# A hybrid retention and attention block: two projections run side by side, two steps moved to GpSimd, the last stage pipelined

## The chip, the cores and the metric

The kernel runs on one core of a Trainium2 chip. A core has five engines that work at the same time: TensorE (PE, matrix products into PSUM), VectorE (DVE), ScalarE (ACT), GpSimd (POOL) and SyncE (SP, which issues most of the DMAs). They are ordered among themselves only by semaphores. The metric is the device time of one execution, in microseconds (us). Lower is better.

## The reference, cut to what matters

One decoder block on `x` of 512 tokens by 1024 columns, in f32:

```
mod = silu(c) @ w_ada + b_ada                    # 6 groups of 1024: sh1 sc1 ga1 sh2 sc2 ga2
h   = rmsnorm(x) * (1 + sc1) + sh1
(retention q, k, v, gate; attention q; compressed k, v; selected k, v; window k, v; 24 gates) = split(h @ w_in)
y_ret = retention(rope(rq), rope(rk), rv) * silu(rg)        # 4 heads, y / rms(y) per head
y_nsa = g0 * o_compressed + g1 * o_selected + g2 * o_window # 8 heads in 2 groups
x = x + ga1 * (concat(y_ret, y_nsa) @ w_out)
h2 = rmsnorm(x) * (1 + sc2) + sh2
x = x + ga2 * ((silu(h2 @ w_gate) * (h2 @ w_up)) @ w_down)
out = rmsnorm(x) * ln_final_g
```

## The kernel before, in words

Tokens are tiled by 128 (TT = 4 tiles), model columns by 128 (KT = 8), FFN columns by 128 (FT = 22). Every large product is made of three fp32r products (`product`: high by high, high by low, low by high), so each weight tile must be split: ACT copies `raw` into `wh` (`high`, L456), POOL subtracts to get `wl` (`low`, L404). The work is counted in units: 24 units of `w_in`, 8 of `w_out`, 44 of gate and up, 22 of down. A unit of `w_in` is two of the eight k tiles (a "quarter") of one of six column chunks. The chunks follow each other: CMP (compressed keys and values, selected keys and values, 512 columns), Q (512), RQK (512), WIN (window keys and values and the gates, 280), RG (512), RV (512). Unit v of the loop `for v in range(U_IN)` is chunk v // 4, quarter v % 4. Each engine has its own copy of this loop, with its side work hung in at fixed v, so the order is written out by hand on every engine, and each engine works strictly in that order.

Quarter q of chunk CMP needs h for k = 2q, 2q+1, and h needs sc1 and sh1 for these columns. So w_ada's first two groups come in quarters: SP streams four `early` tiles and one `w_in` unit per quarter; DVE adds the `early` tiles up with the weights silu(c) (`ada_early`, L713 and L716, 16 operations of 256 columns per quarter); PE sums over partitions (`modulation`, in its queue in the middle of the unit before, ahead of token tile 2); DVE turns the sums into `mods`; ACT makes `hf` (L488) and `hTh` (L491); DVE makes `hTl` (`h_low`, L770); then PE can start the quarter.

The other four groups of w_ada (sc2, ga1, sh2, ga2: operations 16 to 47, one k tile of 1024 columns each, `ada`, L729 and L732) share the ring of seven `raw` tiles with the weight units. `stream()` spreads them over 20 units; DVE works them at v = u - 3 behind the rest of v. `sum_rows` (PE, L1180, one call is two matmuls) gives the rows ga1 and ga2, `mod_rows` (DVE, L765) adds the bias. A raw tile is refilled when its last reader is done.

At set places the evacuated projections are rotated (`rope_chunk`, DVE L808 to L811, per token tile), transposed (`rot_transposes`, PE L1201, L1206), and split again (`rot_high` on ACT, `rot_low` on DVE, L846, L849). `pairs_transposes` (PE) and `pairs_copy` (ACT, L530) lay out the compressed branch, whose small MLP runs behind unit 14 (L1399).

Attention and retention run in 42 slots (`for n in range(SLOTS)`), with tables that name the slot of each side task: scores (PE), exp (ACT), values (PE, L1274), row minima (`row_min`, DVE L875), and
- `add_branch` (DVE L894 to L901): 1/denominator, times gate, `tmpo` from PSUM (L896), then `mix += tmpo` (L901);
- `ret_norm` (DVE): `tmpo` = y * rstd from PSUM (L948), then `mix` = 0.5 * tmpo * gate (L950);
- `mix_transposes` and `out_unit` on PE: `w_out` follows, then the FFN, two matmul groups per f, then the down product.

In the last stage, per token tile: DVE adds the product to `x1` (L1122, two halves), ACT squares with a running sum (L689), DVE makes the variance (L1124, L1125), multiplies the first half by g (L1127), POOL raises to the power -0.5 (L409), DVE scales both halves (L1130, L1131), SP writes 512 KB. DVE does tile t wholly before tile t + 1.

Of the kernel before, what the change touches and what calls it, by code (L numbers as in the profile page):

```python
# [34 lines left out]
CHUNKS = [(C_CMP, 512), (C_Q, 512), (C_RQK, 512), (C_WIN, 280), (C_RG, 512), (C_RV, 512)]  # L35
K_CMP, K_Q, K_RQK, K_WIN, K_RG, K_RV = range(6)
# [46 lines left out]

def stream():

    items = []
    for q in range(UPC):
        items += [("early", 4 * q + j) for j in range(4)] + [("w", q)]
    a = ADA_START
    for u in range(3, UNITS):  # L90
        if u > 3:
            items.append(("w", u))
        upto = min(KT * len(ADA), ADA_START - (-(KT * len(ADA) - ADA_START) * (u - 2) // ADA_UNITS))
        while a < upto:
# [5 lines left out]
def block_kernel(nc, x, c, ln_mix_g, ln_ffn_g, w_ada, b_ada, w_in, cmp_pe_k, cmp_w1_k, cmp_w2_k,  # L100
# [17 lines left out]
    with ExitStack() as ctx:
# [1505 lines left out]
```

## Time and profile before

| | us |
|---|---|
| median of 3 runs | 727.98 |
| lowest and highest | 725.49, 729.76 |
| the profiled execution's own time | 729.54 |
| its span, first to last instruction | 727.7 |

| engine | busy us | share of the span | instructions |
|---|---|---|---|
| PE matmul | 682.1 | 94% | 3547 |
| PE weight load | 564.1 | 78% | 3547 |
| DVE | 332.8 | 46% | 587 |
| POOL | 265.9 | 37% | 127 |
| ACT | 225.5 | 31% | 378 |

How to read it: a matmul's end is modelled and overlaps the next one's start, so PE's busy share says less than the distance from one start to the next. DVE's 46% is a mean: it is over 90% from 60 to 150 us and mostly under 20% in the FFN. "L404" is line 404 of kernel.py. In rows of the timeline the columns are start, duration, engine, line, operation, output<-inputs, their shapes, count, and in brackets the idle time before and who ended it. Rows of the table of stretches are: stretch, its length, then busy us and (count) of PE, PEld, DVE, ACT, POOL (PE and PEld alone where one line was asked for), the granted share of TensorE's clock, the DMA engines' busy share, and GB/s.

### The profile page before, as it was taken

Reading aid. Unit: us, or ns where it says so; the run is one execution under the profiler, and the core shown is the slowest. Engines: PE = TensorE matmul, PEld = TensorE weight load, DVE = VectorE, ACT = ScalarE, POOL = GpSimd, SP = SyncE. Lnnn points to the kernel's source line nnn. Section 1 sums busy time; section 2 is a strip of 40 time slices with the busy share of each in tenths; the row PEclk is TensorE's granted clock in tenths of the full one; section 3 lists DMA queues with packets and bytes.
Section 4 is the critical chain, followed back from the end, with each engine's and each line's share of the span. In section 5 each row is a group of like instructions: output and inputs, shape, how many; then the busy total and the mean of one; then the engine's idle time right before and its main releaser. Section 6 shows DMA issues by size and latency. Waiting matters only on the chain.

```text
span 727.7 us, 9019 instructions
## 1 busy us (share of the span) xinstructions
PE 682.1 (94%) x3547; PEld 564.1 (78%) x3547; DVE 332.8 (46%) x587; ACT 225.5 (31%) x378; POOL 265.9 (37%) x127
## 2 busy tenths in 40 slices
PE   2678899999989898999999999999999999999995
PEld 1556679987768687888898888888888888888884
DVE  4878999977465668152620110000000029633126
ACT  4435233422132333332542222222222213232222
POOL 2316443432000111138034434434434427545531
PEclk9699999999998899999999999999999999999999
DMA  9975986665000000176014233233233223232002
GB/s 314 359 257 152 353 293 234 199 240 228 30 2 1 0 2 1 40 221 202 1 48 127 87 96 107 87 98 104 87 102 101 89 86 117 86 103 72 0 1 116
DMA packets 73962, 88.09 MB, mean 121 GB/s; under 512 B 3048, under 2 KB 57536, under 8 KB 73792
## 3 DMA queue, kind: packets, MB, share of 16 engines
q1 hardware_dynamic: 73184, 86.36, 36.0%
q0 software_dynamic: 416, 1.08, 0.4%
q8 instruction: 28, 0.46, 0.3%
q14 instruction: 14, 0.11, 0.0%
q10 hardware_dynamic: 320, 0.07, 0.0%
HBM read 85.41 MB, written 2.10 MB: 120 GB/s over the span
## 4 chain that ended last, share of the span: by engine, by line
PE 78%; DVE 10%; ACT 3%; issue 3%; DMA 3%; SPq 2%; POOL 0%; POOLq 0%; DVEq 0%
PE ps L1523 11%; PE ps L1524 11%; PE ps L1522 11%; PE ps L1141 11%; PE ps L1143 11%; PE ps L1142 11%; PE ps L1274 3%; DMA raw<-in_w_in 3%; DVE acc L732 2%; DVE ps L875 1%; SPq L344 1%; PE ps L1332 1%; PE ps L1399 1%; PE ps L1228 1%; ACT hf L488 1%
## 5 line engine op out<-in xcount | busy, mean ns | idle before, releaser
L404 POOL TENSOR_TENSOR wl<-raw,wh 128x1024 fp32r<-128x1024 f32 (+1 forms) x94 | 238.6, 2543 | 285.8 <-ACT wh L456 285.6
L456 ACT ACTIVATE wh<-raw 128x1024 fp32r<-128x1024 f32 (+1 forms) x94 | 97.4, 1039 | 154.4 <-PE ps L1524 73.9
L1522 PE MATMUL ps<-hTh,wh 128*128 128x512 f32 (+1 forms) x384 | 142.8, 372 | 0.0
L1523 PE MATMUL ps<-hTl,wh 128*128 128x512 f32 (+1 forms) x384 | 142.6, 371 | 0.0
L1524 PE MATMUL ps<-hTh,wl 128*128 128x512 f32 (+1 forms) x384 | 142.6, 371 | 0.0
L1106 DVE TENSOR_TENSOR act<-ps,sg 128x512 f32<-128x512 f32 x22 | 15.2, 692 | 212.3 <-PE ps L1524 212.3
L1141 PE MATMUL ps<-wh,hTh 128*128 128x512 f32 (+1 forms) x224 | 90.5, 404 | 11.8 <-DVE hTl L770 10.6
L1143 PE MATMUL ps<-wh,hTl 128*128 128x512 f32 (+1 forms) x224 | 85.8, 383 | 0.0
L1142 PE MATMUL ps<-wl,hTh 128*128 128x512 f32 (+1 forms) x224 | 85.7, 383 | 0.0
L1522 PEld LDWEIGHTS ps<-hTh,wh 128*128 128x128 f32 x384 | 72.4, 188 | 12.5
L1523 PEld LDWEIGHTS ps<-hTl,wh 128*128 128x128 f32 x384 | 72.4, 188 | 12.4
L1524 PEld LDWEIGHTS ps<-hTh,wl 128*128 128x128 f32 x384 | 72.4, 188 | 12.4
L1141 PE MATMUL ps<-wh,ah 128*128 128x512 f32 x176 | 68.5, 389 | 0.0
L1142 PE MATMUL ps<-wl,ah 128*128 128x512 f32 x176 | 68.5, 389 | 0.0
L1143 PE MATMUL ps<-wh,al 128*128 128x512 f32 x176 | 68.5, 389 | 0.0
L1141 PEld LDWEIGHTS ps<-wh,hTh 128*128 128x128 f32 x224 | 43.0, 192 | 23.9 <-issue 8.3
L732 DVE SCALAR_TENSOR_TENSOR acc<-raw,cs,acc 128x1024 f32<-128x1024 f32 x28 | 53.3, 1904 | 1.8
L1143 PEld LDWEIGHTS ps<-wh,hTl 128*128 128x128 f32 x224 | 43.0, 192 | 8.3
L1142 PEld LDWEIGHTS ps<-wl,hTh 128*128 128x128 f32 x224 | 43.2, 193 | 7.8 <-issue 1.0
L799 DVE TENSOR_TENSOR raw<-raw,ga 128x1024 f32<-128x1024 f32 x30 | 46.8, 1585 | 0.0
L1101 DVE TENSOR_TENSOR al<-act,ah 128x512 fp32r<-128x512 f32 x22 | 19.5, 888 | 50.5 <-ACT ah L667 50.5
L1274 PEld LDWEIGHTS ps<-V,PT 128*128 128x128 f32 x320 | 38.1, 195 | 5.4 <-DVE tmpo L896 3.2
(197 smaller groups left out, 818.4 us busy)
## 6 DMA issues: line engine op xcount, KB each, us to landing
raw<-in_w_ada SPq DMA_DIRECT2D x32, 512.0 KB, 5.8
raw<-in_w_ff_gate SPq DMA_DIRECT2D x22, 512.0 KB, 3.8
raw<-in_w_ff_up SPq DMA_DIRECT2D x22, 512.0 KB, 3.7
raw<-in_w_ff_down SPq DMA_DIRECT2D x22, 512.0 KB, 3.2
raw<-in_w_in SPq DMA_DIRECT2D x20, 512.0 KB, 7.0
early<-in_w_ada SPq DMA_DIRECT2D x16, 512.0 KB, 9.6
raw<-in_w_out SPq DMA_DIRECT2D x8, 512.0 KB, 6.6
xs<-in_x SPq DMA_DIRECT2D x4, 512.0 KB, 5.3
```

The lines of the kernel that those rows point to most:

```text
L404: pool.tensor_tensor(lo, raw[:, slot, 0:n], hi.bitcast(F32), ALU.subtract).then_inc(w_lo, 1)
L456: a.activation(split(u, n)[0], raw[:, slot, 0:n], ACT.Copy).then_inc(w_hi, 1)
L732: d.scalar_tensor_tensor(dst, raw[:, slot, :], cs[:, k:k + 1], dst, ALU.mult, ALU.add).then_inc(ada_used, 1)
L799: d.tensor_tensor(raw[:, slot, :], raw[:, slot, :], ga[:, :], ALU.mult).then_inc(w_scaled, 1)
L1101: d.tensor_tensor(al[:, f % SPLIT, :], act[:, f, :], ah[:, f % SPLIT, :].bitcast(F32), ALU.subtract).then_inc(a_lo, 1)
L1141: mm(o, ah_, bh_, start=first, stop=False)
L1142: mm(o, ah_, bl_, start=False, stop=False)
L1143: return mm(o, al_, bh_, start=False, stop=last)
L1274: ins = mm(ps[:, 2 + g, h * DE:(h + 1) * DE], PT[:, n % 2, g, h * P:(h + 1) * P], V[:, j, b, g, :], start=j == 0 and h == 0, stop=j == i a ...
L1522: mm(o, hi[:, ks], hTh[:, k, c0:c1], start=k == 0, stop=False)
L1523: mm(o, hi[:, ks], hTl[:, k, c0:c1], start=False, stop=False)
L1524: ins = mm(o, lo[:, ks], hTh[:, k, c0:c1], start=False, stop=k == KT - 1)
```

## The change

The parts are:
1. Chunk WIN now runs with CMP: units 0 to 7 are CMP and WIN in turn for each quarter (`chunk_of`), WIN in PSUM banks 4 and 5, so four chunks follow instead of five. Token tile 3 of WIN is split into two products of 128 and 152 columns for lack of room in one bank. Both units of a quarter's weights are streamed with its `early` tiles. ACT's `high` of the next quarter stands behind the second `hTh`, no longer between the first and the second.
2. `ada_early` takes two tiles in one operation of 512 columns: 8 per quarter instead of 16, each waiting for the one before.
3. Keys of CMP and WIN are rotated together; the transposes of Q and RQK move: the second pair of Q stands behind unit 14 (the unit after the first pair), the MLP follows.
4. Groups sc2, ga1, sh2 of w_ada spread over 14 units from unit 8 on; group ga2 (8 operations) moves to the FFN, one per f from f = 2 to 9, with its `sum_rows` behind gate and up of f = 11 and 12.
5. In attention, `mix += tmpo` and the retention gate are POOL's; POOL's `low` of the first w_out units is put into the slots with them. `add_branch` on DVE stands first in its slot. The retention's factor 0.5 goes into the variance.
6. Last stage: DVE finishes tile t - 1 behind the first half of tile t; the last tile in three pieces; each half is written by its own DMA, one from SP and one from ACT.

The diff, cut to its core ("..." is what is left out):

```diff
-CHUNKS = [(C_CMP, 512), (C_Q, 512), (C_RQK, 512), (C_WIN, 280), (C_RG, 512), (C_RV, 512)]
+CHUNKS = [(C_CMP, 512), (C_WIN, 280), (C_Q, 512), (C_RQK, 512), (C_RG, 512), (C_RV, 512)]
-OUT_AT = {16: 0, 20: 1, 26: 2, 30: 3}
+OUT_AT = {14: 0, 18: 1, 31: 2, 33: 3}
-ADA_UNITS = 20
+ADA_UNITS = 14
+ADA_LAST = 5 * KT
+ADA_FFN = U0_GU + 8
+def chunk_of(u):
+    return (u % 2, u // 2) if u < 2 * UPC else divmod(u, UPC)
...
@@ gpsimd
+            def add_branch(x):
+                i, b = divmod(x, 2)
+                pool.wait_ge(o_read, x + 1)
+                pool.wait_ge(c_mix, i + 1)
+                y = mix[:, i % 2, 512:1024]
+                pool.tensor_tensor(y, y, tmpo[:, :], ALU.add).then_inc(b_mix, 1)
+                pool.wait_ge(b_mix, x + 1)
+            def ret_gate(i):
+                pool.wait_ge(r_half, i + 1)
+                pool.tensor_tensor(mix[:, i % 2, 0:512].rearrange("p (h x) -> p h x", h=RH), normed_y(i),
+                                   rg[:, i, :].rearrange("p (h x) -> p h x", h=RH), ALU.mult).then_inc(r_norm, 1)
+            def attention():
+                for n in range(SLOTS):
+                    if n % 2 and n // 2 in STEP0[1:]:
+                        add_branch(STEP0.index(n // 2) - 1)
+                    if n in SQ_AT:
+                        power(N_RET + SQ_AT[n], yss[:, :])
+                    if n in NORM_AT:
+                        ret_gate(NORM_AT[n])
+                    if n in OUT_AT:
+                        low(U0_OUT + OUT_AT[n])
...
@@ scalar
             for k in range(KT):
-                if k % 2 and k < KT - 1:
-                    high(k // 2 + 1)
...
                 a.activation(hTh[:, k, :], hf[:, k % 2, :], ACT.Copy).then_inc(h_hi, 1)
+                if k % 2 and k < KT - 1:
+                    high(k + 1)
+                    high(k + 2)
...
@@ vector
-                    dst = acc[:, i, 2 * q * P:2 * (q + 1) * P]
-                    src = early[:, j % EARLY, 2 * kk * P:2 * (kk + 1) * P]
+                    dst = acc[:, :, 2 * q * P:2 * (q + 1) * P]
+                    src = early[:, j % EARLY:j % EARLY + 2, 2 * kk * P:2 * (kk + 1) * P]
...
-                d.wait_ge(o_read, x + 1)
-                d.wait_ge(c_mix, i + 1)
-                y = mix[:, i % 2, 512:1024]
-                d.tensor_tensor(y, y, tmpo[:, :], ALU.add).then_inc(b_mix, 1)
-                d.wait_ge(b_mix, x + 1)
...
-                then(d.tensor_tensor(heads_view(tmpo[:, :], RH), heads_view(ps[:, 7, :], RH),
-                                     yss[:, :].unsqueeze(2).broadcast_to([P, RH, RDV]), ALU.mult))
-                d.scalar_tensor_tensor(mix[:, i % 2, 0:512], tmpo[:, :], 0.5, rg[:, i, :], ALU.mult, ALU.mult).then_inc(r_norm, 1)
-                d.wait_ge(r_norm, i + 1)
+                if i:
+                    d.wait_ge(r_norm, i)
+                d.tensor_tensor(normed_y(i), heads_view(ps[:, 7, :], RH),
+                                yss[:, :].unsqueeze(2).broadcast_to([P, RH, RDV]), ALU.mult).then_inc(r_half, 1)
...
-                for n in {7: [0], 10: [1, 2], 12: [3, 4], 19: [9]}.get(v, []):
+                for n in {11: [0, 1], 14: [2, 3], 15: [4, 5]}.get(v, []):
                     rot_low(n)
...
+                if f == 12:
+                    mod_rows(9, ga2, 0, bank=4)
+                if f == 13:
+                    mod_rows(10, ga2, 1, bank=5)
...
             for t in range(TT):
+                last = len(PIECES[t]) - 1
+                take(t, 0)
+                scale_final(t, 0)
+                if t:
+                    finish(t - 1)
+                then(variance_final(t, 0))
...
@@ tensor
-                    pe.wait_ge(rot_lo, min(n - 1, 5))
+                    pe.wait_ge(rot_lo, min(n - 1, 6))
...
-                    pe.wait_ge(r_norm, i)
+                    pe.wait_ge(r_half, i)
...
-                for m in {6: [0], 9: [1, 2], 11: [3, 4], 13: [5, 6], 15: [7, 8], 18: [9]}.get(v, []):
+                for m in {10: [0, 1], 13: [2, 3], 14: [4, 5], 17: [6, 7], 18: [8, 9]}.get(v, []):
                     rot_transposes(m)
...
-                if v == 17:
+                if v == 18:
+                    pe.wait_ge(mod_read, 7)
                     pe.wait_ge(ada_used, ada_ops(5 * KT - 1))
                     sum_columns(0, 40, range(KT)).then_inc(mod_sum, 1)
...
+                if f == 11:
+                    sum_rows(5, 0, bank=4)
+                if f == 12:
+                    pe.wait_ge(mod_read, 9)
+                    sum_rows(5, 1, bank=5)
```

The order on three engines, before and after. First ACT at the start of the projection, before: one weight copy (`wh<-raw`) stands between the two activations of a quarter.

```order
L488 ACTIVATE hf<-xT,mods 128x512
L491 ACTIVATE hTh<-hf 128x512
L456 ACTIVATE wh<-raw 128x1024
L488 ACTIVATE hf<-xT,mods 128x512
L491 ACTIVATE hTh<-hf 128x512
```

ACT after, at the same quarter:

```order
L541 ACTIVATE hf<-xT,mods 128x512
L544 ACTIVATE hTh<-hf 128x512
L541 ACTIVATE hf<-xT,mods 128x512
L544 ACTIVATE hTh<-hf 128x512
L510 ACTIVATE wh<-raw 128x1024
L510 ACTIVATE wh<-raw 128x560
```

The weight copies, now two per quarter, moved behind the second `hTh`.

DVE before, from the last rotated tile of Q to the first two `QTl` (`rot_low`):

```order
L808 TENSOR_TENSOR rt<-stage,cst 128x512
L809 TENSOR_TENSOR rt<-stage,cst 128x8x32
L810 TENSOR_TENSOR rt<-stage,cst 128x8x32
L811 TENSOR_TENSOR rot<-rt 128x2x4x64
L732 SCALAR_TENSOR_TENSOR acc<-raw,cs,acc 128x1024
L849 SCALAR_TENSOR_TENSOR QTl<-ps,QTh 128x4x128 x2
```

DVE after, the same place:

```order
L876 TENSOR_TENSOR rt<-stage,cst 128x512
L877 TENSOR_TENSOR rt<-stage,cst 128x8x32
L878 TENSOR_TENSOR rt<-stage,cst 128x8x32
L879 TENSOR_TENSOR rot<-rt 128x2x4x64
L800 SCALAR_TENSOR_TENSOR acc<-raw,cs,acc 128x1024 x2
L908 SCALAR_TENSOR_TENSOR QTl<-ps,QTh 128x4x128 x2
```

Two `ada` operations stand in front of the first `QTl` where one stood.

POOL before, from the window's last units to the end of attention:

```order
L404 TENSOR_TENSOR wl<-raw,wh 128x1024 x4
L409 TENSOR_TENSOR yss<-yss,expo 128x4 x2
L404 TENSOR_TENSOR wl<-raw,wh 128x1024 x2
L409 TENSOR_TENSOR yss<-yss,expo 128x4
L404 TENSOR_TENSOR wl<-raw,wh 128x1024 x2
L409 TENSOR_TENSOR yss<-yss,expo 128x4
L404 TENSOR_TENSOR wxl<-raw,wxh 128x1024 x4
```

POOL after, the first rows of the same stretch:

```order
L430 TENSOR_TENSOR wl<-raw,wh 128x1024 x2
L435 TENSOR_TENSOR yss<-yss,expo 128x4
L443 TENSOR_TENSOR mix<-mix,tmpo 128x512
L448 TENSOR_TENSOR mix<-hTf,rg 128x512
L443 TENSOR_TENSOR mix<-mix,tmpo 128x512 x2
L435 TENSOR_TENSOR yss<-yss,expo 128x4
L443 TENSOR_TENSOR mix<-mix,tmpo 128x512
L448 TENSOR_TENSOR mix<-hTf,rg 128x512
L430 TENSOR_TENSOR wl<-raw,wh 128x1024 x2
L443 TENSOR_TENSOR mix<-mix,tmpo 128x512
```

Twelve operations of 512 columns (8 `mix<-mix,tmpo`, 4 `mix<-hTf,rg`) are new on POOL, between the powers and the `low` of w_out.

## Rows read from the trace of the kernel before

**Rows 1.** The page: busy time of each engine.

```profile
PE 682.1 (94%) x3547; PEld 564.1 (78%) x3547; DVE 332.8 (46%) x587; ACT 225.5 (31%) x378; POOL 265.9 (37%) x127
```

**Rows 2.** The table of stretches: start-up, projections, attention.

```profile
13.40:66.50 53.10, 39.59 (x160) 29.64 (x161) 43.16 (x88) 24.84 (x39) 16.92 (x7) 0.84 0.80 269
66.50:200.40 133.90, 130.90 (x716) 109.13 (x717) 112.94 (x201) 40.92 (x84) 44.75 (x21) 1.00 0.64 225
200.40:309.50 109.10, 101.69 (x758) 82.66 (x756) 63.45 (x151) 35.57 (x85) 13.55 (x8) 0.94 0.03 8
```

**Rows 3.** Timeline of DVE and ACT in the start-up.

```profile
39.54 1.92 DVE L770 TENSOR_TENSOR hTl<-hf,hTh 128x512 fp32r<-128x512 f32 x1 [0.84 <-ACT hTh L491]
41.38 2.85 DVE L716 SCALAR_TENSOR_TENSOR acc<-early,cs,acc 128x256 f32<-128x256 f32 x7
50.55 0.69 DVE L770 TENSOR_TENSOR hTl<-hf,hTh 128x512 fp32r<-128x512 f32 x1 [0.84 <-ACT hTh L491]
...
59.55 0.69 DVE L770 TENSOR_TENSOR hTl<-hf,hTh 128x512 fp32r<-128x512 f32 x1 [0.68 <-ACT hTh L491]
...
48.10 1.04 ACT L456 ACTIVATE wh<-raw 128x1024 fp32r<-128x1024 f32 x1
```

**Rows 4.** Timeline: DVE beside POOL, with two SBUF inputs and with one.

```profile
140.07 3.52 DVE L732 SCALAR_TENSOR_TENSOR acc<-raw,cs,acc 128x1024 f32<-128x1024 f32 x1
...
140.10 2.40 POOL L404 TENSOR_TENSOR wl<-raw,wh 128x1024 fp32r<-128x1024 f32 x1
...
119.88 1.29 DVE L849 SCALAR_TENSOR_TENSOR QTl<-ps,QTh 128x512 fp32r<-128x512 f32 x2 [0.63 <-ACT QTh L541]
...
119.42 1.40 POOL L404 TENSOR_TENSOR wl<-raw,wh 128x560 fp32r<-128x560 f32 x1 [4.05 <-ACT wh L456]
```

**Rows 5.** Table of stretches, L1141 alone: one 512-column unit, one WIN unit.

```profile
72.44:78.00 5.56, 3.21 (x8) 1.47 (x8) 1.00 0.96 316
118.72:122.00 3.28, 2.40 (x8) 1.47 (x8) 1.00 0.94 335
```

**Rows 6.** Timeline of PE: a sum of rows, the small MLP.

```profile
93.49 1.02 PE L1180 MATMUL ps<-acc,ones 128*128 128x512 f32 x2
...
131.17 8.00 PE L1399 MATMUL ps<-pairsT,w 128*128 128x66 f32 x64
```

**Rows 7.** Waits of PE, 66.5 to 200 us: waiter, releaser, total, times, longest.

```profile
PE ps L1190 <- ACT pairsT L530: 2.0, 1, 2.0
```

**Rows 8.** Timeline of DVE from Q's evacuation to its `rot_low`.

```profile
94.55 0.69 DVE L765 TENSOR_TENSOR ga<-ps,ga 128x512 f32<-128x512 f32 x1
...
95.76 2.62 DVE L809 TENSOR_TENSOR rt<-stage,cst 128x256 f32<-128x256 f32 x1
...
110.39 1.28 DVE L732 SCALAR_TENSOR_TENSOR acc<-raw,cs,acc 128x1024 f32<-128x1024 f32 x1
111.59 1.28 DVE L849 SCALAR_TENSOR_TENSOR QTl<-ps,QTh 128x512 fp32r<-128x512 f32 x2
```

**Rows 9.** Groups by shape, 200.4 to 309.5 us: busy us, mean ns, idle before.

```profile
L404 POOL TENSOR_TENSOR wl<-raw,wh 128x1024 fp32r<-128x1024 f32 x4 | 9.5, 2372 | 38.3 <-ACT wh L456 38.3
...
L901 DVE TENSOR_TENSOR mix<-mix,tmpo 128x512 f32<-128x512 f32 x7 | 4.8, 691 | 0.2
...
L950 DVE SCALAR_TENSOR_TENSOR mix<-tmpo,rg 128x512 f32<-128x512 f32 x4 | 2.8, 692 | 0.1
```

**Rows 10.** The last tile's drain: timeline of PE, DVE and POOL, and the DMA.

```profile
718.49 0.39 PE L1143 MATMUL ps<-wh,al 128*128 128x512 f32 x1
...
719.89 1.28 DVE L1122 TENSOR_TENSOR x<-ps,x 128x512 f32<-128x512 f32 x2
...
722.40 0.92 POOL L409 TENSOR_TENSOR rstd<-rstd,expo 128x1 f32<-128x1 f32 x1 [3.68 <-DVE rstd L1125]
...
723.84 0.74 DVE L1131 SCALAR_TENSOR_TENSOR xb<-x,rstd,gfin 128x512 f32<-128x512 f32 x1
...
out<-xb SPq DMA_DIRECT2D x4, 512.0 KB, 2.6
```

More of the change, by code:

```diff
@@ L87, in stream @@
     for q in range(UPC):
-        items += [("early", 4 * q + j) for j in range(4)] + [("w", q)]
+        items += [("early", 4 * q + j) for j in range(4)] + [("w", 2 * q), ("w", 2 * q + 1)]
     a = ADA_START
-    for u in range(3, UNITS):
-        if u > 3:
+    for u in range(2 * UPC - 1, UNITS):
+        if u >= 2 * UPC:
             items.append(("w", u))
-        upto = min(KT * len(ADA), ADA_START - (-(KT * len(ADA) - ADA_START) * (u - 2) // ADA_UNITS))
+        if u < ADA_FFN:
+            upto = min(ADA_LAST, ADA_START - (-(ADA_LAST - ADA_START) * (u - 2 * UPC + 1) // ADA_UNITS))
+        else:
+            upto = min(KT * len(ADA), ADA_LAST + (u - ADA_FFN) // 2 + 1)
         while a < upto:
@@ L207, in block_kernel @@
         ssq = small("ssq", [P, TT])
-        ssq2 = small("ssq2", [P, TT])
+        part = small("part", [P, 3])
         rstd = small("rstd", [P, TT])
@@ L414, in _ @@
             for u in range(UNITS):
-                for i in {U0_OUT: (0, 1), U0_OUT + 2: (2,), U0_OUT + 4: (3,)}.get(u, ()):
-                    power(N_RET + i, yss[:, :])
+                if u == U0_OUT:
+                    attention()
+                if U0_OUT <= u < U0_OUT + len(OUT_AT):
+                    continue
                 if u == U0_GU + SPLIT:
@@ L1004, in _ @@
                     cmp_scores(0)
-                    mod_rows(9, ga2, 0)
                     for h in range(HPG):
@@ L1010, in _ @@
                     cmp_gates(0)
-                    mod_rows(10, ga2, 1)
                     row_min(2, 0)
@@ L1022, in _ @@
                     ada(j)
-            for h in range(HPG):
-                row_min(3, h)
+            row_min(3, 0)
+            row_min(3, 1)
             cmp_gates(1)
+            row_min(3, 2)
+            row_min(3, 3)
             for n in range(SLOTS):
+                if n % 2 and n // 2 in STEP0[1:]:
+                    add_branch(STEP0.index(n // 2) - 1)
                 for x, h in PAIR_AT.get(n, []):
@@ L1031, in _ @@
                     max_rows(MAX_AT[n])
-                if n % 2 and n // 2 in STEP0[1:]:
-                    add_branch(STEP0.index(n // 2) - 1)
                 if n in CS_AT:
@@ new lines, in scale_final, with variance_final @@
+            def scale_final(t, n):
+                c0, c1 = PIECES[t][n]
+                if t >= 2 and n == 0:
+                    d.wait_ge(out_done[t - 2], 32)
+                d.wait_ge(x2_ok, piece_count(t, n))
+                d.tensor_tensor(xb[:, t % 2, c0:c1], x1[:, t, c0:c1], gfin[:, c0:c1], ALU.mult).then_inc(y_scaled, 1)
+            def variance_final(t, n):
+                d.wait_ge(sq3, piece_count(t, n))
+                v = rstd[:, t:t + 1]
+                if n == 0:
+                    return d.tensor_scalar(v, part[:, 0:1], 1.0 / D, EPS, ALU.mult, ALU.add)
+                return d.scalar_tensor_tensor(v, part[:, n:n + 1], 1.0 / D, v, ALU.mult, ALU.add)
@@ new lines, in finish @@
+            def finish(t):
+                d.wait_ge(rstd_ok, N_X2 + t)
+                d.wait_ge(y_scaled, piece_count(t, 0))
+                d.tensor_scalar(xb[:, t % 2, 0:HALF], xb[:, t % 2, 0:HALF], rstd[:, t:t + 1], None, ALU.mult).then_inc(y_ok, 1)
+            for t in range(TT):
+                last = len(PIECES[t]) - 1
+                take(t, 0)
+                scale_final(t, 0)
+                if t:
+                    finish(t - 1)
+                then(variance_final(t, 0))
+                for n in range(1, last + 1):
+                    take(t, n)
+                for n in range(1, last + 1):
+                    if n == last and last > 1:
+                        then(variance_final(t, 1))
+                    scale_final(t, n)
+                variance_final(t, last).then_inc(var_ok, 1)
@@ L1135, in _ @@
+            finish(TT - 1)
         @block.tensor
```

264 lines of the change are left out of this document (137 added, 127 removed).

## The prediction

> **What bounds the kernel now.** I read the page's busy times first: PE has work for 682.1 of 727.7 us [rows 1], so at most 45 us can be won without taking matmuls away, and no edit takes one away. Then the table of stretches, to see where PE stands still [rows 2]: 13.5 us in the start-up (53.1 less 39.6) at a mean granted clock of 0.84, 3.0 us in the projections, 7.4 us in attention at 0.94, none worth naming in the FFN. The drain is the fourth place: PE's last product starts at 718.49 [rows 10], and the span ends 9 us later. Then the timeline, for what ends PE's waits. In the start-up it is DVE's `hTl` [rows 3]; in attention DVE's `tmpo`, `mix` and row minima. So DVE decides in the start-up and in attention, PE everywhere else, and DVE is nearly full beside the projections: 112.9 of 133.9 us [rows 2].
>
> What makes DVE slow is POOL. `acc<-raw,cs,acc` takes 1.28 us alone [rows 8] and 3.52 us where it starts with a POOL subtraction of 2.40 us [rows 4]: it waits for the whole of it. But two `QTl<-ps,QTh` inside POOL's 119.42 to 120.82 take 0.65 us each [rows 4]: an input from PSUM keeps them free.
>
> This decides whether attention is in danger, and the Trainium skill has the rule ("SBUF — State Buffer", Who interferes with whom): a DVE instruction with at most one SBUF input, outside the two-port modes, does not contend with GpSimd. By that rule, the trace agrees.
>
> **Start-up (parts 1 and 2).** A quarter is 11.0 us on DVE now: from one second `h_low` at 39.54 to the next at 50.55 [rows 3]. The first was held by POOL, 1.92 us instead of 0.69. What changes on this chain: POOL gets a WIN subtraction of 1.40 us [rows 4] in each of four quarters, and DVE, which has no idle time behind `h_low` (seven sums in 2.85 us without a gap), pays it: +5.6. The last CMP subtraction, today held back until all early sums are done, now falls among them: +2.4, of which it costs about 1 already: +1.4. ACT's weight copy of 1.04 us [rows 3] leaves the path between the two halves of three quarters: -3.1. Merged sums: two of 256 columns are 0.81 us (2.85 / 7 each); one of 512 that waits for the one before I put at 0.85, between 0.41 and 1.38 (1.28 and the 0.10 of its wait): 0. Together +3.9: the last half of h, finished at 60.2 today [rows 3], comes at about 64.
>
> PE meanwhile does WIN. A WIN unit is 3.28 us against 5.56 for one of 512 columns [rows 5]. Splitting tile 3 turns 6 products per unit into 12; small ones come every 0.125 us (8.00 / 64 [rows 6]), so a unit is 4.0 us. Behind the last `modulation` (about 60.5) PE still has half a CMP unit and a WIN unit, 6.8 us, so it starts the last quarter at 67, a little after h is there, and is through both units at 76.9. Today the same place in the work is 66.5, the start of unit 4 [rows 2], plus four WIN units that then come later, 13.1: 79.6. Term: **-2.5**. Ends: -8 if the subtractions fall into DVE's waits for ACT as most of the present ones do, +1.5 if each is paid in full and PE stays at the half clock.
>
> **The wait for `pairsT`.** PE stands 2.0 us for ACT's copy [rows 7], because ACT's queue has a weight copy ahead of it whose tile landed late. With eight units fetched ahead of Q, that tile is there. Term: **-2.0** (ends -2 and 0).
>
> **Two waits that come in their place (parts 3 and 4).** Fewer `ada` operations run in the projections (24 instead of 32), but over 14 units instead of 20: 1.7 per unit instead of 1.6, and two consumers moved closer.
>
> (a) Q's second pair of transposes now stands one unit behind the first, and waits for the first `rot_low`. Count from the sum of rows behind Q's last unit (93.49 [rows 6]). PE: 0.9 for the sum, three units of 5.56, eight transposes at 0.125: 18.6. DVE starts 1.06 later and takes 17.04 us to `QTl` today (94.55 to 111.59 [rows 8]), with three `ada` operations between. Now there are four (+1.4), and the subtractions beside it are all 1024 wide where two were 560 (2.40 against 1.40: +2.0); with `QTl`'s own 0.65 that is 22.1. PE waits 3.5. Today it has two more units' time there.
>
> (b) The sum for sh2 needs `ada` operation 39 behind unit 18; it was done four units ahead of its use, now DVE does it in the place of unit 18 itself. From the evacuation of RQK: four tiles to rotate (2.0 each, what is left of the 17.04 when L765, three `ada` and 4.35 of blocking are taken out), five `ada` at 1.38, a dozen small operations at 0.2 (an estimate, under L765's 0.69), four subtractions that block 2.3 each: 26.5, begun 3.5 before unit 15 ends: 23. PE: three units, two sets of transposes, two sums: 20. PE waits 3.
>
> Together 6.5; but POOL subtracts only as fast as PE frees slots, so a standing PE takes blocking off DVE. I take **+5.5**; ends 0 (POOL's work falls into DVE's own waits) and +10 (the subtractions win every tie).
>
> **ga2 in the FFN (part 4).** The two sums of rows cost the same there. PE gets rid of about 0.5 us of waiting in units 21 and 22. In the FFN the second sum waits for `mod_rows` of the first, and DVE does this only behind `act` of f = 12, which needs the last product: 0.69 + 0.69 + handing over, +1.5, with nothing to cover it. The eight `ada` cost DVE up to 3.5 us each [rows 4] of a round of two units, 11 us [rows 5], in which it has one product and little else: hidden, and `act` is wanted only a round later. SP's fetch of g waits for that `mod_rows`, and behind it unit 34 of gate and up; that is needed four units later, 20 us: hidden. Term **+1.0** (ends 0, +2).
>
> **Attention (part 5).** DVE loses 8 x 0.72 (L901, 0.69 and its wait) and 4 x 0.72 (L950) [rows 9]: 8.6 us of 63. In the places where PE waits for DVE all of it counts, elsewhere none. Putting `add_branch` ahead of `row_min` helps the values and hurts the next pair by the same 1.1 us, since PE needs both: 0. `cmp_out`'s products wait for half the norm: inside the 8.6. Against it: POOL's twelve operations. POOL does 1024 columns in 2.37 us [rows 9], so 512 in about 1.25, against 0.69. Nobody waits for them at once: tile 0's mixing is transposed two slots (5 us) behind its last addition, the last tile's behind 24 products of w_out (5.5 us). DVE's operations there read PSUM, but for the tiny ones, so they aren't held [rows 4]. I take half of 8.6: **-4.5**; ends 0 and -9, since two half-clock spells (the 0.94) may also go.
>
> The Trainium skill advises against the move ("GPSIMD Engine Reference", Engine selection: elementwise work of two inputs belongs on VectorE, about two times slower on GpSimd). The ratio is in the rows (512 columns in an estimated 1.25 on POOL, from 2.37 for 1024, against 0.69). If the rule held for the path, twelve times 0.56 us would be added instead of taken away; that is rival C.
>
> **The drain (part 6).** Today DVE reaches the last tile at 719.89, a microsecond behind PE's end, since its round is longer than PE's, and ends at 724.6; the 512 KB take 2.6 [rows 10]. After: DVE keeps up; from PE's end at 718.9: the last half in two pieces, 0.7; squares 0.45 + 0.2 for the last; variance 0.2; POOL 0.92; scaling by ACT 0.63; steps between, 0.6: issue at 722.6, end 725.4 instead of 727.5. **-2.1** (ends -1, -3).
>
> **Sum.** -2.5 - 2.0 + 5.5 + 1.0 - 4.5 - 2.1 = **-4.6**. The profiled execution's own time is 729.5, which is 1.6 above the median; taken off it, 724.9, and off the median of 727.98, **723.4**.
>
> **Rivals.**
> A. DVE isn't late. (a) and (b) don't arise, the start-up gives 6 and attention 8: -2 - 6 + 1 - 8 - 2.1 = -17: 711. For it: nothing on PE waits for DVE between 95 and 118 today. Against: DVE's slack there is under a microsecond.
> B. Slower: the shared port. Place: units 12 to 18. Once POOL's subtractions, each 2.4, alternate with DVE's sums at every turn, (a) and (b) cost 10, the start-up +1.5, attention nothing: -2 + 1.5 + 10 + 1 + 0 - 2.1 = +8.4: 736. It decides from (a) + (b) above 9.
> C. Attention isn't shortened: POOL's operations become the last thing waited for at `mix_transposes` and `tmpo`'s reuse, 12 x 0.56 less 4 hidden, or PE's own queue and ACT's exp take the place: -0.1 + 2 to -0.1: 728 to 730.
> D. The merged sums and the new order do nothing, and only the drain and `pairsT` are won, with (a) at 3.5: 727; I count it with C.
>
> **Chances.** The forecast 0.50, A 0.20, B 0.13, C and D 0.17. The forecast's own range is 719 to 728; A reaches to 711, B to 736; two in ten are left outside 712 to 732. A measurement of this kernel tells a change of about 0.5%, 3.6 us: faster is under 724.3, slower over 731.6. Of the forecast 0.32 is faster and 0.18 the same; A is faster; B is slower; of C and D 0.03, 0.10 and 0.04. Faster 0.55, same 0.28, slower 0.17.
>
> **What will show it.** Start-up: unit 8's first product near 77 us; over 80 refutes that term. (a): a wait of PE for `QTl` or its transposes behind unit 14 of 2 to 5 us; (b): one for `acc` behind unit 18. The wait for `pairsT` under 0.5. Attention: the stretch from its first scores to the last values shorter by 2 to 7 us; if it isn't, C. FFN: one wait of 1.5 us at f = 12. Drain: 6.5 us from PE's last product to the end. If PE waits for DVE nowhere in the projections, A is right.

## The result and the profile after

The changed kernel takes 753.18 us (median; 750.82 to 755.01), the kernel before on the same chip 727.43: a ratio of 1.0354, 95% interval 1.0311 to 1.0396. It is 3.5% slower; the forecast was 723.4, within 712 to 732. Ratios leave out an execution that lies over 1.5% above the fastest of its kernel; of all those below this is one, of 731.25 us, of the kernel with slots 31 and 33.

The page of the changed kernel: busy times, and the granted clock of TensorE in 40 slices.

```profile
PE 706.4 (94%) x3571; PEld 587.2 (78%) x3571; DVE 332.9 (44%) x530; ACT 228.2 (30%) x384; POOL 281.7 (37%) x139
...
PEclk9699997797999969959999999999999999999999
```

PE is busy for 24.3 us more than in [rows 1], with 24 more matmuls, all small. The work hasn't grown, it runs slower: the second row dips in five slices behind the start-up, to 5 and 6 tenths in two of them. In the kernel before there is one such dip, of two slices:

```profile
PEclk9699999999998899999999999999999999999999
```

The table of stretches of the changed kernel. The columns: start and end, length, busy time of PE, PEld, DVE, ACT and POOL, granted clock, DMA share, GB/s. The stretches are the start-up to unit 8's first product, the projections, attention, w_out with h2, the FFN to PE's last product.

```profile
13.40:75.05 61.65, 52.89 (x281) 45.16 (x281) 51.84 (x61) 30.01 (x51) 22.95 (x13) 0.86 0.85 289
75.05:213.30 138.25, 129.59 (x625) 106.99 (x624) 90.44 (x174) 36.59 (x72) 36.14 (x16) 0.90 0.45 158
213.30:333.00 119.70, 110.87 (x750) 90.78 (x750) 58.58 (x137) 34.66 (x84) 28.35 (x19) 0.85 0.05 17
333.00:388.60 55.60, 55.41 (x282) 46.70 (x282) 24.81 (x39) 21.42 (x35) 24.16 (x13) 0.98 0.40 117
388.60:746.60 358.00, 356.55 (x1638) 297.24 (x1637) 100.85 (x105) 98.57 (x130) 164.39 (x65) 1.00 0.32 97
```

The clock is 0.90 in the projections, where it was 1.00, and 0.85 in attention against 0.94 [rows 2]. The same view over the four longest spells:

```profile
123.93:140.99 17.06, 17.06 (x74) 16.29 (x73) 3.82 (x5) 1.96 (x6) 2.96 (x2) 0.50 0.41 151
168.30:178.50 10.20, 9.09 (x29) 7.87 (x30) 1.82 (x3) 0.77 (x2) 0.00 (x0) 0.50 0.29 104
270.70:284.35 13.65, 13.35 (x63) 11.50 (x63) 4.44 (x14) 0.42 (x1) 0.27 (x1) 0.50 0.01 1
318.50:335.50 17.00, 17.00 (x72) 14.62 (x69) 1.07 (x3) 2.17 (x4) 3.48 (x3) 0.50 0.46 169
```

In each the clock is 0.50, that is 1.2 GHz, and PE has work for 56.5 of the 57.9 us. Half of that, 28 us, is lost. Two more spells of 3.4 us each lie in attention. The kernel before has two spells behind its start-up, of 6.8 us each. (The Trainium skill, "TensorE: Matmul & The Clock Gate", Part 1, has the clock at half after PE has been idle; behind the two waits of 4.0 us below this trace agrees, and the third experiment tests it at the first of them.)

What stands ahead of each spell is in the waits of PE (waiter, releaser, us in total, times, longest), for the projections, attention and the FFN:

```profile
PE ps L1297 <- issue: 4.0, 1, 4.0
PE ps L1246 <- DVE acc L800: 4.0, 1, 4.0
...
PE ps L1407 <- DVE mcol L934: 4.2, 4, 2.1
PE ps L1364 <- DVE tmpo L957: 1.5, 1, 1.5
...
PE ps L1272 <- DVE ga L833: 1.4, 1, 1.4
```

L1297 is the second pair of Q's transposes. The view names no releaser for it, but DVE's timeline shows one: L908, `QTl`, ends at 123.2 as a pair, its first half at 122.6, and the transposes start at 122.7. L1246 is the sum for sh2. These are the forecast's waits (a) and (b). The wait of 2.1 for `mcol` ends at 271.0, that of 1.5 for `tmpo` at 316.2. From the first scores to the last transposes of h2 PE's waits sum to 9.0 us, in the kernel before to 7.4; there the longest is 1.1. The four spells begin 1.2 us behind (a)'s end, 1.1 us before (b)'s, 0.3 us before the third's and 2.3 us behind the last one's.

DVE's timeline ahead of (a), with the columns start, length, engine, line, operation:

```profile
108.31 4.83 DVE L800 SCALAR_TENSOR_TENSOR acc<-raw,cs,acc 128x1024 f32<-128x1024 f32 x2
...
113.99 2.61 DVE L878 TENSOR_TENSOR rt<-stage,cst 128x256 f32<-128x256 f32 x1
...
119.38 2.67 DVE L800 SCALAR_TENSOR_TENSOR acc<-raw,cs,acc 128x1024 f32<-128x1024 f32 x2
121.96 1.28 DVE L908 SCALAR_TENSOR_TENSOR QTl<-ps,QTh 128x512 fp32r<-128x512 f32 x2
```

DVE has no gap there. L878 takes 0.42 us alone; beside a subtraction of POOL it takes 2.61, as in [rows 8]. Ahead of (b) it is otherwise:

```profile
152.63 0.17 DVE L806 TENSOR_TENSOR mods<-ps,cols 128x8 f32<-128x8 f32 x1 [4.99 <-PE ps L1246]
...
165.93 3.33 DVE L800 SCALAR_TENSOR_TENSOR acc<-raw,cs,acc 128x1024 f32<-128x1024 f32 x1
```

DVE itself stood idle for 5.0 us, because `mod_columns(7)`, which needs PE's sum behind unit 16, is ahead of the rotation of RQK's tiles 2 and 3 in its queue. The last row is operation 39; PE goes on when it is done.

In attention, DVE and POOL ahead of the two waits:

```profile
266.83 2.08 DVE L954 TENSOR_TENSOR rgt<-rgt,gates 128x8 f32<-128x8 f32 x1
...
266.51 2.37 POOL L430 TENSOR_TENSOR wl<-raw,wh 128x1024 fp32r<-128x1024 f32 x1 [9.30 <-ACT wh L510]
...
313.91 1.22 DVE L867 TENSOR_TENSOR raw<-raw,ga 128x1024 f32<-128x1024 f32 x1
315.05 0.20 DVE L953 RECIPROCAL rgt<-ps 128x8 f32<-128x8 f32 x1
315.28 0.17 DVE L954 TENSOR_TENSOR rgt<-rgt,gates 128x8 f32<-128x8 f32 x1
```

A product of 8 columns takes 2.08 us instead of 0.17, because POOL subtracts a tile of w_out beside it. That is slot 18 of `OUT_AT`. Before the last values, slot 33 puts a scaling of 1.22 us ahead of `add_branch`.

The start-up, and the drain's last rows:

```profile
62.99 0.69 DVE L838 TENSOR_TENSOR hTl<-hf,hTh 128x512 fp32r<-128x512 f32 x1 [0.68 <-ACT hTh L544]
...
746.60 0.39 PE L1235 MATMUL ps<-wh,al 128*128 128x512 f32 x1
...
748.86 0.55 POOL L435 TENSOR_TENSOR rstd<-rstd,expo 128x1 f32<-128x1 f32 x1 [3.58 <-DVE rstd L1202]
```

### The profile page after: what moved, and what is told of

Same layout as the page of the kernel before. It is cut to its first block, busy times and chain, and to the rows that moved or that the text cites. A ratio compares the mean times of both kernels' runs of the same rounds, so it can differ in the third digit from the quotient of the medians.

```text
span 753.2 us, 9013 instructions
## 1 busy us (share of the span) xinstructions
PE 706.4 (94%) x3571; PEld 587.2 (78%) x3571; DVE 332.9 (44%) x530; ACT 228.2 (30%) x384; POOL 281.7 (37%) x139
## 4 chain that ended last, share of the span: by engine, by line
PE 85%; DVE 8%; issue 4%; ACT 1%; DMA 1%; SPq 0%; POOL 0%; DVEq 0%; POOLq 0%; ACTq 0%
PE ps L1233 12%; PE ps L1235 12%; PE ps L1234 12%; PE ps L1620 11%; PE ps L1619 11%; PE ps L1618 11%; PE ps L1364 5%; DVE acc L784 3%; PE ps L1497 2%; PE ps L1421 2%; PE ps L1246 1%; DVE ps L934 1%; PE ps L1318 1%; PE ps L1338 1%; DMA xs<-in_x 1%
## 5 line engine op out<-in xcount | busy, mean ns | idle before, releaser
L430 POOL TENSOR_TENSOR wl<-raw,wh 128x1024 fp32r<-128x1024 f32 x94 | 239.8, 2556 | 296.8 <-ACT wh L510 296.6
L510 ACT ACTIVATE wh<-raw 128x1024 fp32r<-128x1024 f32 x94 | 97.3, 1038 | 145.9 <-PE ps L1620 74.0
L1233 PE MATMUL ps<-wh,hTh 128*128 128x512 f32 (+2 forms) x232 | 93.4, 402 | 2.9 <-DVE hTl L838 2.9
L1234 PE MATMUL ps<-wl,hTh 128*128 128x512 f32 (+2 forms) x232 | 90.0, 388 | 0.0
L1235 PE MATMUL ps<-wh,hTl 128*128 128x512 f32 (+2 forms) x232 | 89.8, 387 | 0.0
L1618 PEld LDWEIGHTS ps<-hTh,wh 128*128 128x128 f32 x384 | 72.4, 188 | 12.8 <-issue 0.5
L1233 PEld LDWEIGHTS ps<-wh,hTh 128*128 128x128 f32 x232 | 46.2, 199 | 12.1 <-issue 3.7
L1235 PEld LDWEIGHTS ps<-wh,hTl 128*128 128x128 f32 x232 | 45.9, 198 | 8.7
L1158 DVE TENSOR_TENSOR al<-act,ah 128x512 fp32r<-128x512 f32 x22 | 28.3, 1288 | 50.6 <-ACT ah L725 50.6
L800 DVE SCALAR_TENSOR_TENSOR acc<-raw,cs,acc 128x1024 f32<-128x1024 f32 x28 | 48.3, 1723 | 1.2
L1364 PEld LDWEIGHTS ps<-V,PT 128*128 128x128 f32 x320 | 44.0, 220 | 5.1 <-issue 2.6
```

Source lines behind the costliest of these rows:

```text
L430: pool.tensor_tensor(lo, raw[:, slot, 0:n], hi.bitcast(F32), ALU.subtract).then_inc(w_lo, 1)
L510: a.activation(split(u, n)[0], raw[:, slot, 0:n], ACT.Copy).then_inc(w_hi, 1)
L800: d.scalar_tensor_tensor(dst, raw[:, slot, :], cs[:, k:k + 1], dst, ALU.mult, ALU.add).then_inc(ada_used, 1)
L1158: d.tensor_tensor(al[:, f % SPLIT, :], act[:, f, :], ah[:, f % SPLIT, :].bitcast(F32), ALU.subtract).then_inc(a_lo, 1)
L1233: mm(o, ah_, bh_, start=first, stop=False)
L1234: mm(o, ah_, bl_, start=False, stop=False)
```

## Experiments

Theory T: each new wait of PE is paid twice, as the wait and as a spell at half clock beside or behind it; take the waits away and the change gains. Rivals: R, the clock falls for another reason; S or U, a mend only moves the wait; P, POOL's operations make attention longer. All ratios are to the kernel before, with their 95% intervals. Line numbers in waits are those of each kernel's own file.

**Q's second pair of transposes one unit later.**

```diff
-for m in {10: [0, 1], 13: [2, 3], 14: [4, 5], 17: [6, 7], ...   # PE
+for m in {10: [0, 1], 13: [2, 3], 15: [4, 5], 17: [6, 7], ...
```

ACT's `rot_high` and DVE's `rot_low` of this pair follow, to units 16 and 17.

> The changed kernel with Q's second pair of transposes (tiles 2 and 3) one unit later, behind unit 15 as the kernel before has two units more for it; nothing else moved. Theory T (a wait of PE of 4 us is paid twice, once as the wait and once more as the stretch at half clock that follows it): the wait of 4.2 us behind unit 14 and the 17.1 us at 1.2 GHz behind it both go, 4.2 + 8.5 = 12.7 less: about 740.5. Rival R (the clock falls for another reason, the matmuls of the MLP or the moment in the program): only the wait goes, the stretch at half clock stays: 749. Rival S (DVE's work is merely moved, the sum for sh2 behind unit 18 waits longer in turn): 750 to 753.

739.1 us, ratio 1.0128 (1.0083 to 1.0172). Of the two long waits in the projections one is left, and the stretch in which the MLP stands has its clock back:

```profile
PE ps L1246 <- DVE acc L800: 4.0, 1, 4.0
```

```profile
118.00:152.00 34.00, 34.00 (x201) 29.74 (x200) 30.06 (x38) 9.27 (x17) 10.75 (x6) 1.00 0.69 235
157.30:166.30 9.00, 9.00 (x29) 7.84 (x30) 0.85 (x2) 0.69 (x2) 0.00 (x0) 0.50 0.32 118
```

The MLP isn't what brings the clock down, which is one form of R; the spell at (b) stays with its wait.

**DVE's order at unit 17.**

```diff
-if v == 17:
-    mod_columns(7, ...)
 ...
     rope_chunk(v // UPC - 2, ...)
+if v == 17:
+    mod_columns(7, ...)
```

> The changed kernel with DVE's mod_columns(7) put behind the rotation of RQK's tiles 2 and 3 (it stands ahead of it and holds DVE for 5.0 us until PE's sum behind unit 16 is there). Theory T: DVE reaches ada operation 39 4 us earlier, the wait behind unit 18 (4.3 us) falls under 0.5 and the 10.2 us at half clock behind it go too: 4.3 + 4.4 = 8.7 less, about 744.5. Rival R (clock falls anyway): 749. Rival S (DVE's count of work sets the wait, not the order): a wait of 3 to 4 us stays, 752 to 753.

741.61 us, 1.0149 (1.0089 to 1.0208). The mirror image: (a) is left with its 4.0 us and 20 us at half clock, (b) is gone with its spell. The gain is larger than T's, which had 744.5, and part of it is luck: in the profiled execution attention's spells are shorter, 20.4 us instead of 37.6, though PE's waits of 2.1 and 1.5 us there are as before. The last row is attention, with a clock of 0.91 where the changed kernel has 0.85.

```profile
121.70:141.70 20.00, 20.00 (x83) 18.98 (x84) 5.96 (x9) 2.48 (x6) 2.95 (x2) 0.50 0.44 150
142.00:200.00 58.00, 57.33 (x312) 46.67 (x311) 37.22 (x104) 14.41 (x27) 13.26 (x6) 1.00 0.36 127
...
204.97:321.50 116.53, 106.80 (x762) 86.94 (x762) 59.66 (x140) 34.66 (x84) 29.40 (x20) 0.91 0.05 16
```

**The wait filled, not shortened.**

```diff
+if v == 14:
+    pe.wait_ge(mod_read, 6)
+    for j in range(17):
+        mm(ps[:, 7, :], hTh[:, j % KT, 0:P], hTh[:, j % KT, :], start=True, stop=True)
```

> The changed kernel with 17 products of 512 columns (17 x 0.227 = 3.9 us) whose results nobody reads, on PE between unit 14 and Q's second pair of transposes, where it stands idle for 4.2 us. The wait isn't shortened, only filled. Theory T: no stretch at half clock behind it, 8.5 us less: about 744.7. Rival R (the clock falls for another reason): 753. If DVE and POOL were slowed by it: over 753.

743.34 us, 1.0182 (1.0165 to 1.0198). PE does 4.0 us of useless work, the transposes come no earlier (10.5 us behind the first pair, as in the changed kernel), and the kernel is some 12 us faster; its four executions (741.6 to 743.9) all lie below the changed kernel's lowest, 750.8. This is the run that separates T from R: same program, same place, same DVE; only the idleness is gone, and with it the spell. From the transposes to the first scores the profiled execution takes 49.9 us instead of 58.6, 8.7 less against T's 8.5; the rest of the 12 lies in attention, whose spells were shorter here, 23.9 us instead of 37.6, behind the same waits. The rows: the fill and the transposes, then the stretches behind unit 14, around (b), which was not filled, and attention:

```profile
120.92 4.01 PE L1479 MATMUL ps<-hTh 128*128 128x512 f32 x17
125.09 1.12 PE L1297 MATMUL ps<-cst,rot 128*128 128x128 f32 x7 [0.16 <-issue]
...
121.60:131.00 9.40, 9.24 (x63) 8.20 (x62) 8.22 (x10) 1.88 (x3) 0.00 (x0) 1.00 0.73 237
131.00:148.00 17.00, 17.00 (x101) 14.60 (x101) 10.18 (x12) 5.09 (x9) 6.26 (x4) 1.00 0.51 169
160.00:180.00 20.00, 16.00 (x73) 13.31 (x72) 9.47 (x28) 6.71 (x13) 4.74 (x2) 0.83 0.26 97
...
206.97:326.10 119.13, 109.25 (x764) 90.05 (x764) 59.62 (x140) 34.66 (x84) 29.62 (x20) 0.90 0.08 28
```

**The slots of w_out's tiles.** `OUT_AT = {16: 0, 20: 1, 26: 2, 30: 3}`, as before the change, and nothing else.

> The changed kernel with OUT_AT, the slots of attention in which w_out's first four tiles are scaled and split, as before (16, 20, 26, 30 for 14, 18, 31, 33). Theory T: the scaling of 1.22 us that stands ahead of the last add_branch goes, PE's wait of 1.9 us for tmpo at 314 shrinks to some 0.6 and the 17.1 us at half clock behind it (318.5 to 335.6) go: 1.3 + 8.5, about 743; the waits for row minima at 261 and 268 stay or move. Rival P (attention is longer because of POOL's twelve operations): 752 to 754, the spell stays.

735.9 us, 1.009 (1.0072 to 1.0108): some 19 us better than the changed kernel where 10 were expected, because both waits of attention go, not the one of 1.5 alone. P is refuted.

```profile
PE ps L1407 <- DVE mcol L934: 2.3, 4, 0.9
PE ps L1318 <- DVE mcol L934: 2.2, 2, 1.1
...
PE ps L1364 <- DVE tmpo L957: 0.4, 1, 0.4
```

**The same slots in the kernel before.**

```diff
-OUT_AT = {16: 0, 20: 1, 26: 2, 30: 3}
+OUT_AT = {14: 0, 18: 1, 31: 2, 33: 3}
```

> The kernel before with OUT_AT alone as in the changed kernel (14, 18, 31, 33), nothing else. If the slots do harm by themselves (a scaling of 1.22 us ahead of the last add_branch, POOL's subtraction of 2.4 us ahead of the last power): a wait of PE of 1.5 to 2 us before the last scores and a stretch at half clock behind it, 3 to 10 us slower than the kernel before. Rival (they do harm only together with POOL's new operations): within 1 us of it.

742.2 us, 1.0173 (1.0138 to 1.0208). This one line costs the kernel before 13 us. Here the first slot meets the norm: PE waits 2.8 us for `mix` beside a subtraction, then 1.5 for `tmpo` at the end, and the profiled execution has 17 and 24 us at half clock behind them.

```profile
PE ps L1307 <- DVE mix L950: 3.3, 2, 2.8
PE ps L1274 <- DVE tmpo L896: 3.2, 4, 1.5
```

**The three mends together**, then two halves of `OUT_AT` on top of the other two mends.

> The changed kernel with three mends together: Q's second pair of transposes behind unit 15, mod_columns(7) behind the rotation of RQK's tiles 2 and 3, OUT_AT as before. Theory T (the loss is these waits and the half clock behind them, and the rest of the change pays): PE waits nowhere over 0.5 us between 60 and 165; from the 753.2 us of the changed kernel's span go 4.2 + 4.3 + 12.9 in the projections and 18 in attention (as in the run with OUT_AT alone): 714, ratio to the kernel before 0.980. Rival U (each mend only moves the wait to the next place, the gains don't add): 725 to 730, ratio about 1.

720.42 us, 0.9889 (0.9866 to 0.9911): faster than the kernel before, and between T's 714 and U's 725, since (b) isn't quite gone; 1.6 us of it are left with a spell of 6.8 us in the profiled execution. With (a) out of the way PE is early at (b).

By the ratios the three mends give 16.5, 14.9 and 19.2 us one at a time, 51 together, and 34 at once. The gains don't add. In part U is right: the 1.6 us at (b) stand there only when (a) is mended too. In part the executions with one mend also had shorter spells behind waits that they left alone, as seen above; in the profiled execution with `OUT_AT` alone the wait of 4.0 us at (a) has 3.4 us at half clock beside it instead of 17.1. The single runs show where each gain lies, its size only to some 5 us: the first is 16.5 by the ratios and 12.1 between the profiled executions.

> The kernel with Q's transposes and mod_columns(7) mended, and of OUT_AT only the first two slots as changed (14, 18, 26, 30). If POOL's subtraction of 2.4 us at slot 18 holds DVE's product with the gates (2.08 us instead of 0.17 in the changed kernel): a wait of 2 us for mcol and the half clock behind it, 4 to 9 us over the 720.4 of the kernel with the three mends. If only the last two slots do harm: 720 to 721.

729.37 us, 1.0006 (0.998 to 1.0032). The wait for `mcol` is back, 2.1 us.

> The same with only the last two slots as changed (16, 20, 31, 33). If the scaling of 1.22 us ahead of the last add_branch is the harm: a wait of 1.7 us for tmpo before the last values and up to 17 us at half clock behind it, 5 to 10 us over 720.4. If only the first two do harm: 720 to 721.

722.17 us, 0.9901 (0.9869 to 0.9934). The wait for `tmpo` is back, 1.5 us, and the profiled execution has 17 us at half clock behind it, but the five executions range from 720.1 to 731.3. By the ratios the first pair of slots costs 8.5 us, the second 0.9, which lies within the intervals: in three of its five executions the second pair costs next to nothing (under 2 us), in two 8 to 11 us.

**Who does attention's additions.** The kernel with the mends, POOL's twelve operations on DVE again:

```diff
+d.tensor_tensor(y, y, tmpo[:, :], ALU.add).then_inc(b_mix, 1)        # in DVE's add_branch
+d.tensor_tensor(mix[:, i % 2, 0:512]..., normed_y(i), rg[:, i, :]..., ALU.mult).then_inc(r_norm, 1)
```

> The same three mends, but the twelve operations of attention that went to POOL (eight additions of a branch, four products with the retention gate) on DVE again, in the changed kernel's order. If the move to POOL shortens attention as the forecast has it (half of 8.6 us): 4 to 5 us more than the kernel with the three mends. Rival C of the forecast (DVE isn't what decides there): the same within 1 us. Rival K (DVE 1 us late at ten places brings the clock down more often): 6 to 12 us more.

731.85 us, 1.0047 (1.0019 to 1.0075), 11.4 us more. The twelve executions fall into two groups of six, 728.3 to 729.4 and 734.3 to 735.8, and the median lies between them. K holds: the waits for row minima grow from 0.9 and 1.1 to 1.5 and 2.0 us, and the clock falls.

```profile
PE ps L1408 <- DVE mcol L930: 3.2, 3, 1.5
PE ps L1319 <- DVE mcol L930: 2.0, 1, 2.0
```

```profile
197.40:368.00 170.60, 162.41 (x1030) 134.65 (x1027) 88.11 (x187) 56.01 (x119) 36.38 (x20) 0.91 0.17 50
```

The same stretch with the operations on POOL:

```profile
198.40:353.70 155.30, 148.69 (x1029) 123.47 (x1026) 80.91 (x174) 55.95 (x119) 51.68 (x32) 1.00 0.19 55
```

The move alone, made in the kernel before:

> The kernel before with part 5's move alone: the eight additions of a branch and the four products with the retention gate on POOL, OUT_AT and the order of row minima as they are. If the move itself pays: attention and w_out together 4 to 5 us shorter than the 162.1 us of before, and its two stretches at half clock (6.8 us each, 3.1 us lost) may go: 720 to 724 against 728. Rival C of the forecast (not shortened): 727 to 729. Rival K (each wait on DVE is paid twice by the clock, as the kernel with the mends and all on DVE, 11.4 us slower, makes likely): 716 to 720.

722.91 us, 0.9925 (0.9901 to 0.9948). It pays 5 us by itself. In the profiled executions the stretch of 162.5 us (first scores to the last transposes of h2) becomes 155.2; PE's waits in it sum to 5.3 us instead of 7.4, and 3.4 us are at half clock instead of 13.6. So 2.1 us of the 7.3 are waits and up to 5.1 are the clock. C is refuted in both kernels.

**Row minima ahead of `add_branch` again**, beside the three mends.

> The same three mends, and in attention DVE's row minima ahead of add_branch again, as in the kernel before. If the new order put the row minima late: PE's waits for mcol at about 219, 240 and 276 of the run with OUT_AT alone (1.5, 1.5 and 1.3 us, 0.2 of each the step itself) go, 2 to 3 us less than the kernel with the three mends. Rival (the forecast's step: helps one and hurts the other by the same 1.1 us): waits for tmpo of 1 us come in their place at the next values, the same time within 1 us.

718.46 us, 0.9856 (0.9832 to 0.988). 2.0 us less; the executions don't overlap (717.3 to 718.7 against 719.4 to 722.0), though the intervals of the ratios do. The forecast had the order as neutral; it isn't. Waits for `tmpo` come back (4, of 0.6 at most), those for `mcol` shrink, ahead of scores from 1.1 to 0.3, and all of PE's waits in this stretch sum to 5.3 us instead of 6.7.

**Two mends more: the best version.**

```diff
 if f == 12:
-    pe.wait_ge(mod_read, 9)
     sum_rows(5, 1, bank=5)
 ...
-if v == 18:
-    compressed()
 for j in ada_after.get(v + 3, []):
     ada(j)
+if v == 18:
+    compressed()
```

> The kernel with the three mends and the row minima ahead (718.5 us), and two more: PE's second sum of rows for ga2 in the FFN without its wait for mod_rows of the first (they use different banks), and DVE's compressed() behind the ada operation of unit 18 instead of ahead of it. Theory T: the wait of 1.6 us in the FFN goes; operation 39 ends 2.7 us earlier, so the wait of 1.7 us behind unit 18 goes with the stretch at half clock of 3.4 us behind it: 1.6 + 1.7 + up to 1.6 less, about 714. Rival: compressed() is late instead (PE waits for kcr behind unit 19), 716 to 718.

713.17 us, 0.9794 (0.9769 to 0.9818): 2.1% faster than the kernel before, and near T's 714. Its page, and its stretches with the same bounds in the work as those of the changed kernel above:

```profile
PEclk9989999999999999999999999999999999999999
```

```profile
76.54:194.60 118.06, 117.39 (x627) 96.69 (x626) 94.10 (x171) 36.38 (x72) 34.54 (x16) 1.00 0.53 185
194.60:294.20 99.60, 94.44 (x751) 78.15 (x750) 56.10 (x140) 34.77 (x84) 28.45 (x19) 1.00 0.03 9
294.20:348.60 54.40, 54.21 (x282) 45.76 (x281) 24.85 (x39) 21.42 (x35) 24.13 (x13) 1.00 0.47 141
348.60:704.90 356.30, 356.30 (x1639) 297.26 (x1637) 100.86 (x105) 98.61 (x130) 164.43 (x65) 1.00 0.33 98
```

PE's longest wait behind the start-up is 1.1 us, and there is no spell between the start-up and the drain.

## Why the prediction was wrong

The places of the two new waits in the projections were right and their sizes nearly so. What failed is what a wait costs, and one line of the change that got no term.

- **Start-up, -2.5.** Measured -4.6: unit 8's first product starts at 75.05 against 79.6. The last half of h is there at 63.7, forecast 64. PE came to the last quarter at 65.9 instead of 67, and a WIN unit took it 3.6 us instead of 4.0. (The forecast's own 76.9 and 79.6 are 2.7 apart, not 2.5.)
- **`pairsT`, -2.0.** The wait is gone; that this is because the tile had landed was not tested.
- **(a) and (b), 3.5 and 3.0.** 4.0 and 4.0. (a) has the forecast's cause, DVE full and held by POOL. (b) has another: the forecast counted a chain of 23 us of work and missed that `mod_columns(7)`, moved to unit 17, makes DVE wait 5.0 us for PE in the middle of it. Reordering alone took the wait away while (a) stood; with (a) mended too 1.6 us were left, and they went when `compressed()` moved behind the operation, which is order again.
- **Together +5.5: the step that failed.** The forecast priced a wait at its length. The spells at (a) and (b) cost about half of their PE time, 17.1 / 2 + 9.1 / 2 = 13.1, more than the waits' 8.0. Beyond the start-up the forecast used the clock of [rows 2] only as something that attention might give back.
- **ga2, +1.0.** The FFN grew by 3.5 us (354.5 to 358.0): two sums of rows at 0.9, which the projections no longer have, and a wait of 1.4 at f = 12, forecast 1.5. That stands: less the small waits of the projections, 1.0 us before and 0.7 now, it is +1.1.
- **Attention, -4.5.** With w_out it is 175.3 us against 162.5, +12.8. The move to POOL is worth what the forecast gave it, 5 us (0.9925 alone), and 11.4 where DVE is nearly late. That the size came out is luck: the forecast took half of DVE's 8.6 us as wait taken off PE, and PE's waits shrank by 2.1; most of the rest is clock, which the forecast had put at the end of its range. The step that failed here: the new `OUT_AT` stood in the diff and got no term. It costs 13 us in the kernel before. The mechanism was in the forecast, [rows 4]; it was applied to the projections and not to attention, where it said that DVE's operations read PSUM "but for the tiny ones, so they aren't held": the tiny one was held for 2.08 us. (Of the two `QTl` of [rows 4] only the first lies wholly inside POOL's subtraction; that is enough for the reading that an input from PSUM goes free.) The step "putting `add_branch` ahead of `row_min`: 0" is wrong by 2.0.
- **Drain, -2.1.** From the start of PE's last product to the end 6.6 us against 9.2: -2.6. From that product's end it is 6.2, where the forecast had 6.5.

Of the rivals B came nearest: its mechanism is what happens at (a), and it priced both waits at 10 us, against 8.0; but its 736 has neither the clock nor `OUT_AT` in it. Without the clock, the profiled executions give -4.6 - 2.0 + 8.0 + 1.1 + 1.6 - 2.6 = +1.5, where 1.6 is by how much PE's waits in attention grew, `OUT_AT`'s two among them; the forecast's sum was -4.6. The rest is the clock: behind the start-up and ahead of the drain the changed kernel spends 64.8 us at 1.2 GHz, the kernel before 13.7, and half of the difference is 25.6. This is an upper bound, since PE isn't busy in all of it. The two make 27.1; the changed kernel's span is 25.5 longer. So the loss is the clock's nearly whole, and the gains and the new waits about cancel.

What stays open: why a wait of 2.0 us for `pairsT` leaves the clock of the kernel before alone, and one of 1.5 before the last values doesn't. (In the run with the kernel before and the new slots the wait for `pairsT` was 2.7 us, with 3.4 us at half clock behind it.) Nor did a long wait stand ahead of the two spells of 6.8 us in the kernel before, where no wait in attention is over 1.1 us, while the best version has one of 1.1 us in attention and no spell. The runs show that all this happens, not what decides between the cases.

## What to carry to other kernels

A wait of PE of more than a microsecond or two in a full stretch is to be priced at itself and at a risk for the clock: here half of 3.4 to 20.5 us behind a wait of 4.0, half of up to 17 behind one of 1.5, nothing behind one of 2.0. So a change that opens two such waits can lose all that its other parts gain, and one that closes them gains more than the trace's idle time promises. Before a wait is bought off with less work, look at the order of the queue that it waits for: three of the six mends here moved one statement. Every moved number in a table of slots needs its own term: what on the other engines meets the operation in its new slot.

## What was not expected of the hardware

- The spells at half clock behind the same wait differ in length: behind (a) 17.1 us in the changed kernel, 20.5 in the run with `mod_columns(7)` moved, 3.4 in the run with `OUT_AT` alone.
- Kernels with long waits scatter, and the granted clock mostly scatters with the time: the kernel with slots 14 and 18 took 722.3 to 731.8 us over 10 executions, with granted clocks from 0.994 to 0.967; the one without long waits 711.2 to 714.4.
- 17 useless products in place of an idle PE made the kernel 12.5 us faster by the ratios (1.0354 against 1.0182), 8.7 of it in the trace between the filled wait and the first scores. The fill itself costs nothing, since it lies in the wait.
- A DVE operation with 8 columns, both inputs in SBUF, waits until POOL's subtraction ends, like one with 1024: 2.08 us instead of 0.17.
